# Turning x ahead of the first products over three bank pairs, and dummy products on PE at two places

## The chip, the cores and the metric

The kernel runs on one core of one Trainium2 chip. The metric is the device time of one execution in microseconds (us), the median of several runs. Engines are named as in the profile: PE is TensorE (PEld its weight loads), DVE is VectorE, ACT is ScalarE, POOL is GpSimd, SP is SyncE, which here only issues DMAs. An engine name with a q (PEq, ACTq) is that engine's sequencer.

## The reference

One layer of a decoder trunk, for a prompt of 256 tokens and 8 samples of one token each (264 columns in all), width 2048, all in float32:

```
x = x + 0.5 * SwiGLU_1(RMSNorm(x))          # 2048 -> 5632 twice, and back
h = RMSNorm(x);  P = h @ w_in               # 2048 -> 6400: attention, RWKV-7, gated conv
x = x + concat(attention, rwkv, conv) @ w_out
x = x + 0.5 * SwiGLU_2(RMSNorm(x))
```

The attention part is dilated sliding-window attention with 8 heads over cached keys and values. The RWKV-7 part is a delta-rule scan over the tokens with a state of 64x64 for each of 12 heads. After the scan each head's output `y` goes through a group norm (mean and variance over the 64 channels of the head), gets a per-head bonus added and is multiplied with a gate:

```
y = (y - mean(y)) * rsqrt(var(y) + 64e-5) * ln_w + ln_b
y_rwkv = (y + sum(r * k * r_k) * v) * g
```

Two ends of this matter here: the very beginning, where x is brought in and turned, and the end of the group norm, behind which the products with `w_out` start.

## The kernel before, in words

x is kept with its 2048 features on the partitions (16 tiles of 128) and the 264 tokens as columns, in `xr`. Every weight product is made in three passes, so that it is as exact as float32: weights and activations are each split into a head (`wH`, `xH`, rounded to fp32r, made by ACT) and a tail (`wL`, `xL`, the rest, made by DVE), and PE adds head x head, head x tail and tail x head (lines 324 to 326 in `products`). Weights come as chunks of four tiles of 128 rows by 256 columns (512 KB) through a ring of four buffers: SP's queue loads `raw` (line 297 in `load`), ACT makes the head (line 305 in `head`), DVE the tail (line 311 in `tail`), and PE has 24 products of 264 columns per chunk. The semaphores `tail_made` and `chunk_used` count chunks and let each stage run up to four chunks ahead.

The order of work of each engine is written out by hand, one program per engine, and each engine does its own in order.

The start. x comes from memory with tokens on the partitions (`xin`, four pieces of 512 features, and `xsin` for the samples), and PE turns it: `pe_turn_x(q)` transposes two tiles of features into two PSUM banks, with two large transposes (line 890) and a small one for the samples (line 891) each, against the identity in `cb`. There are eight such pairs q = 0 to 7. DVE copies a pair to `xr` (line 898 in `copy`), ACT makes its heads `xH` (line 359 in `x_heads`), DVE its tails `xL` (line 367 in `x_tails`). The two bank pairs 4, 5 and 6, 7 are used in turn, so turn q waits for the copy of pair q - 2; an even q also waits for its piece of x. ACT's queue loads four groups of small vectors (line 836), then `cb` (line 837) and `xsin` (line 838). SP's queue loads the four pieces of x (line 853), each followed by one weight chunk. PE turns pairs 0 to 3 (and the vectors, line 877), makes the first chunk of products, turns 4 and 5, makes the second chunk, turns 6 and 7, and goes on with the third.

The norm. x is normalised only after the product (a column of the result is scaled with the root of its sum of squares), so the sum of squares is not needed at first. ACT squares each pair (line 352 in `squares`), from behind the first four weight heads on, into two slots. POOL adds the squares up (lines 824 and 822 in `pool_squares`), one pair after the other. PE's `norm_sum` (lines 385 and 386) adds over the partitions with a matrix of ones. It stands behind the sixth chunk of the first pair of column tiles, and waits until POOL has added all eight pairs. ACT's root (393), DVE's reciprocal (398) and the first scaled gate (404) follow.

From there on, and in all the later projections, the products run as a stream.

The group norm's end. It works on two groups of columns: part 0 is the first 128, part 1 the other 136. PE sums over a head (2053), squares and sums (2064), spreads the root over the head's channels (2073); DVE centres, multiplies and adds in place in PSUM (2102 to 2105), ACT makes the mix's heads (2137) and DVE its tails (2141). PE's last piece of work there is `pe_group_spread` of part 1 (2073) and six transposes of the final state (2034), which ACT copies out (2190) behind two weight heads of the output projection. Then PE waits for the first weight tail of the output projection. The bonus sums of part 1 lie in banks 4 and 5 and are read by DVE's `dve_bonus_values` (2124), which counts `bonus_made`. The first products of the output projection write banks 4 and 5 too.

Of the kernel before, what the change touches and what calls it, by code (L numbers as in the profile page):

```python
# [23 lines left out]
P = 128  # L24
# [86 lines left out]
def build(nc, t, o):  # L111
# [597 lines left out]
    def pe_ffn(pe, u, gu, dn):  # L709
        w = 2 * u  # L710

        def gate_up(i, first_pair):
            for k in range(GU_PER):
# [4 lines left out]
                if k == 4 and not first_pair:  # L718
                    pe.wait_ge(S("up_scaled"), FT // 2 * u + i)
                products(pe, xH, xL, CK * (k % 4), CK, 0 if k < 4 else 2, k % 4 == 0, k % 4 == 3,  # L720
                         gu, GU_PER, i, k)
                if first_pair and u == 0 and k < 2:
                    pe_turn_x(pe, 2 * k + 4)
                    pe_turn_x(pe, 2 * k + 5)
                if first_pair and k == (5 if u == 0 else 3):
# [107 lines left out]
    def act_start(act):  # L833
        for name, r, n in (("ffn1_norm", "ffn1", 16), ("mix_norm", "mix", 16), ("ffn2_norm", "ffn2", 16),
                           ("rwkv_mu", "mu", 20)):
            act.dma_start(vrowa[VA[r]:VA[r] + n, :], row_view(name)).then_inc(S("base_in"), 16)
        act.dma_start(cb[:], t["c_base"]).then_inc(S("base_in"), 16)
        act.dma_start(xsin[:], t["x_sample"].rearrange("b s f -> (b s) f")).then_inc(S("x_in"), 16)
        act.wait_ge(S("constants_set"), 3)
        nc.scalar.activation(sd[:, 0:1], ep, ACT.Square)  # L840
        act.wait_ge(S("vectors_a_set"), 1)
        for k in range(RING):
            x_heads(act, 0, 2 * k)
            x_heads(act, 0, 2 * k + 1)
            head(act, CK, GU1, GU_PER, 0, k, fresh=True)
# [3 lines left out]
    def sp_start(sp):  # L849
        xp = t["x_prompt"][0].rearrange("(b p) f -> p b f", p=P)  # L850
        for k in range(RING):
            cols = slice(k * CK * P, (k + 1) * CK * P)
# [19 lines left out]

    def pe_start(pe):
        pe.wait_ge(S("base_in"), 16 * 5)
        pe.wait_ge(S("x_in"), 32)
        pe_turn_x(pe, 0)
        nc.tensor.transpose(ps[:, 0, 0:68], vrowa[:], ident[0:68, 0:68]).then_inc(S("vectors_a_turned"), 1)
        pe_turn_x(pe, 1)
        pe_turn_x(pe, 2)
        pe_turn_x(pe, 3)  # L880

    def pe_turn_x(pe, q):

        if q >= 2:
            pe.wait_ge(S("x_ready"), q - 1)
        if q % 2 == 0 and q:
            pe.wait_ge(S(X_IN[q // 2]), 16)
        for d in (2 * q, 2 * q + 1):
            for b in range(2):
                nc.tensor.transpose(ps[:, 4 + d % 4, b * P:b * P + P], xin[:, b, d * P:d * P + P], ident)  # L890
            last = nc.tensor.transpose(ps[:, 4 + d % 4, T:N], xsin[:, d * P:d * P + P], ident[0:NB, 0:NB])
        last.then_inc(S("x_turned"), 1)

    def dve_start(dve):
        def copy(q):
            dve.wait_ge(S("x_turned"), q + 1)
            b = 4 + 2 * (q % 2)
            nc.vector.tensor_copy(xr[:, 2 * q:2 * q + 2, :], ps[:, b:b + 2, 0:N]).then_inc(S("x_ready"), 1)
        copy(0)
        dve.wait_ge(S("vectors_a_turned"), 1)  # L900
        nc.vector.tensor_copy(vcol[:, 0, :], ps[:, 0, 0:68]).then_inc(S("vectors_a_set"), 1)
        dve.wait_ge(S("vectors_a_set"), 1)
        for k in range(RING):
            copy(2 * k + 1)
            x_tails(dve, 0, 2 * k)
            if k < RING - 1:
                copy(2 * k + 2)
            x_tails(dve, 0, 2 * k + 1)
# [1061 lines left out]
    def pe_chunks(pe):  # L1970
# [58 lines left out]
        pe_group_squares(pe, 1)  # L2029
        pe_group_spread(pe, 1)  # L2030
        pe.wait_ge(S("states_out"), 4)
        pe.wait_ge(S("head_root"), 3)
        for j in range(RT):
            last = nc.tensor.transpose(pf[0:C, 1024 + j * P:1024 + j * P + P], ST[:, j, :], ident)
        last.then_inc(S("state_turned"), 1)

    GROUP = ((slice(0, P), 0, 2), (slice(P, N), 6, 3))
# [352 lines left out]
```

## Time and profile before

| | us |
|---|---|
| median of 3 runs | 2142.46 (2138.77 to 2144.42) |
| the profiled execution | 2135.76 |
| its span, first to last instruction | 2133.9 |
| PE busy | 2076.6 (97%), weight loads 2042.1 |
| DVE, ACT, POOL busy | 1170.6 (55%), 880.8 (41%), 191.9 (9%) |
| mean granted TensorE clock | 0.992 of full |

A row of the windows gives the length of a stretch, then for each engine its busy time and in brackets how many instructions ran in it. A row of the timeline merges what repeats: start, time taken, engine, line, operation, output and inputs, how many, and in square brackets how long the engine was idle before it and what released it. A row of the waits sums up who waited for whom.

### The profile page before, as it was taken

Reading aid. Unit: us, or ns where it says so; the run is one execution under the profiler, and the core shown is the slowest. Engines: PE = TensorE matmul, PEld = TensorE weight load, DVE = VectorE, ACT = ScalarE, POOL = GpSimd, SP = SyncE. Lnnn points to the kernel's source line nnn. Section 1 sums busy time; section 2 is a strip of 40 time slices with the busy share of each in tenths; the row PEclk is TensorE's granted clock in tenths of the full one; section 3 lists DMA queues with packets and bytes.
Section 4 is the critical chain, followed back from the end, with each engine's and each line's share of the span. In section 5 each row is a group of like instructions: output and inputs, shape, how many; then the busy total and the mean of one; then the engine's idle time right before and its main releaser. Section 6 shows DMA issues by size and latency. Waiting matters only on the chain.

```text
span 2133.9 us, 44654 instructions
## 1 busy us (share of the span) xinstructions
PE 2076.6 (97%) x18392; PEld 2042.1 (96%) x18392; DVE 1170.6 (55%) x1203; ACT 880.8 (41%) x1004; POOL 191.9 (9%) x160
## 2 busy tenths in 40 slices
PE   6999999999999999999997979999999999999999
PEld 5999999999999999999985879999999999999999
DVE  4555555555545445568996555655555555544443
ACT  4443444434434434434345444444444444433333
POOL 3000000000000000014401860000000000000000
PEclk9999999999999999999998999999999999999999
DMA  5556555555555556668872045555555656556553
GB/s 162 178 179 185 178 184 179 178 186 177 182 173 178 187 170 198 177 201 219 245 229 61 4 153 183 179 181 181 182 178 180 183 179 184 178 162 201 181 182 123
DMA packets 361374, 373.41 MB, mean 175 GB/s; under 512 B 13321, under 2 KB 353837, under 8 KB 361190
## 3 DMA queue, kind: packets, MB, share of 16 engines
q1 hardware_dynamic: 352128, 350.33, 52.8%
q0 software_dynamic: 5424, 15.39, 3.0%
q10 hardware_dynamic: 3742, 6.52, 0.9%
q8 instruction: 62, 1.02, 0.2%
q14 instruction: 18, 0.15, 0.0%
HBM read 366.89 MB, written 5.32 MB: 174 GB/s over the span
## 4 chain that ended last, share of the span: by engine, by line
PE 88%; DVE 6%; DMA 2%; ACT 1%; issue 1%; POOL 1%; ACTq 1%; POOLq 0%; SPq 0%; DVEq 0%
PE ps L324 28%; PE ps L326 28%; PE ps L325 28%; DVE wL L311 2%; DMA raw<-in_w_in_dram 2%; POOL acc L822 1%; DMA vb<-in_cache_swa_v_dram 0%; PE ps L1878 0%; ACTq L1246 0%; PE ps L1875 0%; PE ps L1886 0%; PE ps L1186 0%; DMA xsin<-in_x_sample_dram 0%; DVE ss L1339 0%; ACT wH L305 0%
## 5 line engine op out<-in xcount | busy, mean ns | idle before, releaser
L311 DVE TENSOR_TENSOR wL<-raw,wH 128x1024 fp32r<-128x1024 f32 (+1 forms) x676 | 830.1, 1234 | 847.6 <-ACT wH L305 847.0
L305 ACT ACTIVATE wH<-raw 128x1024 fp32r<-128x1024 f32 (+1 forms) x676 | 699.8, 1037 | 979.6 <-PE ps L326 899.4
L324 PE MATMUL ps<-xH,wH 128*128 128x264 f32 x3616 | 1032.2, 285 | 8.8 <-DVE wL L311 8.7
L325 PE MATMUL ps<-xL,wH 128*128 128x264 f32 x3616 | 1028.9, 285 | 0.0
L326 PE MATMUL ps<-xH,wL 128*128 128x264 f32 x3616 | 1028.8, 285 | 0.0
L324 PEld LDWEIGHTS ps<-xH,wH 128*128 128x128 f32 x3616 | 683.1, 189 | 13.7 <-issue 12.6
L326 PEld LDWEIGHTS ps<-xH,wL 128*128 128x128 f32 x3616 | 682.7, 189 | 0.0
L325 PEld LDWEIGHTS ps<-xL,wH 128*128 128x128 f32 x3616 | 682.3, 189 | 0.2
L324 PE MATMUL ps<-hH,wH 128*128 128x264 f32 x1408 | 402.4, 286 | 0.0
L326 PE MATMUL ps<-hH,wL 128*128 128x264 f32 x1408 | 401.5, 285 | 0.0
L325 PE MATMUL ps<-hL,wH 128*128 128x264 f32 x1408 | 401.3, 285 | 0.0
L324 PEld LDWEIGHTS ps<-hH,wH 128*128 128x128 f32 x1408 | 265.0, 188 | 0.2
L325 PEld LDWEIGHTS ps<-hL,wH 128*128 128x128 f32 x1408 | 265.1, 188 | 0.0
L326 PEld LDWEIGHTS ps<-hH,wL 128*128 128x128 f32 x1408 | 264.6, 188 | 0.0
L324 PE MATMUL ps<-mixH,wH 128*128 128x264 f32 x256 | 73.6, 287 | 7.4 <-DVE wL L311 7.4
L325 PE MATMUL ps<-mixL,wH 128*128 128x264 f32 x256 | 73.4, 287 | 0.0
L326 PE MATMUL ps<-mixH,wL 128*128 128x264 f32 x256 | 73.3, 286 | 0.0
L408 ACT ACTIVATE st<-gt 128x528 f32<-128x528 f32 x44 | 28.5, 647 | 83.5 <-DVE gt L404 83.5
L822 POOL TENSOR_TENSOR acc<-acc,sq 128x528 f32<-128x528 f32 x21 | 34.1, 1622 | 287.4 <-ACT sq L352 286.4
L324 PEld LDWEIGHTS ps<-mixH,wH 128*128 128x128 f32 x256 | 48.9, 191 | 7.6 <-DVE wL L311 7.6
L824 POOL COPY acc<-sq 128x528 f32<-128x528 f32 x3 | 2.9, 973 | 574.5 <-ACT sq L352 574.5
L326 PEld LDWEIGHTS ps<-mixH,wL 128*128 128x128 f32 x256 | 48.9, 191 | 0.0
(365 smaller groups left out, 1030.1 us busy)
## 6 DMA issues: line engine op xcount, KB each, us to landing
raw<-in_ffn_w_gate_dram SPq DMA_DIRECT2D x176, 512.0 KB, 3.5
raw<-in_ffn_w_up_dram SPq DMA_DIRECT2D x176, 512.0 KB, 3.5
raw<-in_ffn_w_down_dram SPq DMA_DIRECT2D x128, 512.0 KB, 3.5
raw<-in_w_in_dram SPq DMA_DIRECT2D x100, 512.0 KB, 4.8
raw<-in_ffn_w_down_dram SPq DMA_DIRECT2D x64, 384.0 KB, 3.1
raw<-in_w_out_dram SPq DMA_DIRECT2D x32, 512.0 KB, 4.3
kb<-in_cache_swa_k_dram POOLq DMA_DIRECT2D x24, 256.0 KB, 6.5
vb<-in_cache_swa_v_dram ACTq DMA_DIRECT2D x24, 256.0 KB, 6.8
```

The costliest lines, as they stand in the source:

```text
L305: nc.scalar.activation(wH[:, k % RING, 0:nk, :], raw[:, k % RING, 0:nk, :], ACT.Copy).then_inc(S("head_made"), 1)
L311: nc.vector.tensor_tensor(wL[:, k % RING, 0:nk, :], raw[:, k % RING, 0:nk, :], wH[:, k % RING, 0:nk, :].bitcast(F32), ALU.subtract).then_i ...
L324: nc.tensor.matmul(out, wH[:, k % RING, q, cols], high, start=a, stop=False)
L325: nc.tensor.matmul(out, wH[:, k % RING, q, cols], low, start=False, stop=False)
L326: last = nc.tensor.matmul(out, wL[:, k % RING, q, cols], high, start=False, stop=b)
L408: nc.scalar.activation(st[:], gt[:], ACT.Silu).then_inc(S("silu_made"), 1)
L822: nc.gpsimd.tensor_tensor(acc[:], acc[:], sq[:, slot, :, :], ALU.add).then_inc(S("squares_added"), 1)
L824: nc.gpsimd.tensor_copy(acc[:], sq[:, 0, :, :]).then_inc(S("squares_added"), 1)
```

## The change

- The loads of `cb` and `xsin` leave ACT's queue and stand first on SP's, ahead of the pieces of x.
- PE starts with 32 dummy products of ones (256 columns of bfloat16, into bank 4), as soon as POOL has set the constants.
- PE turns pairs 0 to 5 ahead of the first chunk of products, and 6 and 7 behind it; nothing stands behind the second chunk. The turns use three bank pairs (2 and 3, 4 and 5, 6 and 7) in turn, so turn q waits for the copy of pair q - 3. DVE's copies are one pair further ahead of its tails.
- Behind the last spread of the group norm PE makes 8 dummy products, after a wait for DVE's bonus values, and 36 more behind the transposes of the state.

The dummies' results are never read. The whole diff:

```diff
--- before.py
+++ after.py
@@ -719,9 +719,9 @@
                     pe.wait_ge(S("up_scaled"), FT // 2 * u + i)
                 products(pe, xH, xL, CK * (k % 4), CK, 0 if k < 4 else 2, k % 4 == 0, k % 4 == 3,
                          gu, GU_PER, i, k)
-                if first_pair and u == 0 and k < 2:
-                    pe_turn_x(pe, 2 * k + 4)
-                    pe_turn_x(pe, 2 * k + 5)
+                if first_pair and u == 0 and k == 0:
+                    pe_turn_x(pe, 6)
+                    pe_turn_x(pe, 7)
                 if first_pair and k == (5 if u == 0 else 3):
                     norm_sum(pe, w)
 
@@ -834,8 +834,6 @@
         for name, r, n in (("ffn1_norm", "ffn1", 16), ("mix_norm", "mix", 16), ("ffn2_norm", "ffn2", 16),
                            ("rwkv_mu", "mu", 20)):
             act.dma_start(vrowa[VA[r]:VA[r] + n, :], row_view(name)).then_inc(S("base_in"), 16)
-        act.dma_start(cb[:], t["c_base"]).then_inc(S("base_in"), 16)
-        act.dma_start(xsin[:], t["x_sample"].rearrange("b s f -> (b s) f")).then_inc(S("x_in"), 16)
         act.wait_ge(S("constants_set"), 3)
         nc.scalar.activation(sd[:, 0:1], ep, ACT.Square)
         act.wait_ge(S("vectors_a_set"), 1)
@@ -848,6 +846,8 @@
 
     def sp_start(sp):
         xp = t["x_prompt"][0].rearrange("(b p) f -> p b f", p=P)
+        sp.dma_start(cb[:], t["c_base"]).then_inc(S("base_in"), 16)
+        sp.dma_start(xsin[:], t["x_sample"].rearrange("b s f -> (b s) f")).then_inc(S("x_in"), 16)
         for k in range(RING):
             cols = slice(k * CK * P, (k + 1) * CK * P)
             sp.dma_start(xin[:, :, cols], xp[:, :, cols]).then_inc(S(X_IN[k]), 16)
@@ -871,40 +871,54 @@
                 pool.dma_start(vrowb[VB[r]:VB[r] + 1, a * C:a * C + C], t[name]).then_inc(S("vectors_b_in"), 16)
 
     def pe_start(pe):
+        pe.wait_ge(S("constants_set"), 3)
+        pe_warm(4, 32)
         pe.wait_ge(S("base_in"), 16 * 5)
         pe.wait_ge(S("x_in"), 32)
         pe_turn_x(pe, 0)
         nc.tensor.transpose(ps[:, 0, 0:68], vrowa[:], ident[0:68, 0:68]).then_inc(S("vectors_a_turned"), 1)
-        pe_turn_x(pe, 1)
-        pe_turn_x(pe, 2)
-        pe_turn_x(pe, 3)
+        for q in range(1, 6):
+            pe_turn_x(pe, q)
+
+    def pe_warm(bank, count):
+
+        for _ in range(count):
+            nc.tensor.matmul(ps[:, bank, 0:2 * P], ones[:].bitcast(BF16)[:, 0:P], ones[:].bitcast(BF16),
+                             start=True, stop=True)
+
+    def turned_banks(q):
+
+        return 2 + q % 3 * 2
 
     def pe_turn_x(pe, q):
 
-        if q >= 2:
-            pe.wait_ge(S("x_ready"), q - 1)
+        if q >= 3:
+            pe.wait_ge(S("x_ready"), q - 2)
         if q % 2 == 0 and q:
             pe.wait_ge(S(X_IN[q // 2]), 16)
         for d in (2 * q, 2 * q + 1):
+            bank = turned_banks(q) + d % 2
             for b in range(2):
-                nc.tensor.transpose(ps[:, 4 + d % 4, b * P:b * P + P], xin[:, b, d * P:d * P + P], ident)
-            last = nc.tensor.transpose(ps[:, 4 + d % 4, T:N], xsin[:, d * P:d * P + P], ident[0:NB, 0:NB])
+                nc.tensor.transpose(ps[:, bank, b * P:b * P + P], xin[:, b, d * P:d * P + P], ident)
+            last = nc.tensor.transpose(ps[:, bank, T:N], xsin[:, d * P:d * P + P], ident[0:NB, 0:NB])
         last.then_inc(S("x_turned"), 1)
 
     def dve_start(dve):
         def copy(q):
             dve.wait_ge(S("x_turned"), q + 1)
-            b = 4 + 2 * (q % 2)
+            b = turned_banks(q)
             nc.vector.tensor_copy(xr[:, 2 * q:2 * q + 2, :], ps[:, b:b + 2, 0:N]).then_inc(S("x_ready"), 1)
         copy(0)
         dve.wait_ge(S("vectors_a_turned"), 1)
         nc.vector.tensor_copy(vcol[:, 0, :], ps[:, 0, 0:68]).then_inc(S("vectors_a_set"), 1)
         dve.wait_ge(S("vectors_a_set"), 1)
+        copy(1)
         for k in range(RING):
-            copy(2 * k + 1)
+            if k < RING - 1:
+                copy(2 * k + 2)
             x_tails(dve, 0, 2 * k)
             if k < RING - 1:
-                copy(2 * k + 2)
+                copy(2 * k + 3)
             x_tails(dve, 0, 2 * k + 1)
             tail(dve, CK, GU1, GU_PER, 0, k)
 
@@ -2028,11 +2042,14 @@
         pe_bonus(pe, 1)
         pe_group_squares(pe, 1)
         pe_group_spread(pe, 1)
+        pe.wait_ge(S("bonus_made"), 3)
+        pe_warm(4, 8)
         pe.wait_ge(S("states_out"), 4)
         pe.wait_ge(S("head_root"), 3)
         for j in range(RT):
             last = nc.tensor.transpose(pf[0:C, 1024 + j * P:1024 + j * P + P], ST[:, j, :], ident)
         last.then_inc(S("state_turned"), 1)
+        pe_warm(4, 36)
 
     GROUP = ((slice(0, P), 0, 2), (slice(P, N), 6, 3))
```

## Rows read from the trace of the kernel before

**Rows 1.** the page's chain that ended last, share of the span by engine

```profile
PE 88%; DVE 6%; DMA 2%; ACT 1%; issue 1%; POOL 1%; ACTq 1%; POOLq 0%; SPq 0%; DVEq 0%
```

**Rows 2.** the waits, 0 to 60 us: us in total, times, longest us

```profile
PE ps L890 <- DMA xsin<-in_x_sample_dram: 10.3, 1, 10.3
...
PE ps L324 <- DVE wL L311: 5.4, 4, 1.8
...
PE ps L385 <- POOL acc L822: 4.7, 1, 4.7
```

**Rows 3.** windows: stretch and length; busy us (instructions) by engine; PEclk, DMA share, GB/s

```profile
10.00:17.50 7.50, 6.72 (x25) 3.84 (x25) 4.40 (x9) 3.60 (x7) 0.00 (x0) 1.00 0.84 287
18.20:22.50 4.30, 4.25 (x24) 4.29 (x24) 1.32 (x3) 1.87 (x3) 0.00 (x0) 1.00 0.40 122
...
46.20:50.90 4.70, 0.00 (x0) 0.00 (x0) 2.86 (x2) 2.87 (x3) 4.41 (x4) 0.75 0.36 112
50.90:55.30 4.40, 4.40 (x16) 3.98 (x17) 1.72 (x1) 1.76 (x2) 4.40 (x9) 0.50 0.47 127
...
1252.90:1260.20 7.30, 0.02 (x1) 0.00 (x0) 6.13 (x7) 3.25 (x5) 6.64 (x4) 0.54 0.00 0
1260.20:1263.70 3.50, 3.42 (x15) 3.42 (x16) 2.39 (x3) 1.62 (x3) 0.09 (x1) 0.50 0.78 213
1263.70:1267.10 3.40, 3.40 (x30) 3.40 (x29) 1.72 (x2) 1.77 (x2) 1.27 (x2) 1.00 0.97 297
```

**Rows 4.** the chain that ended last, in order of time: start us, us, what

```profile
33.21 0.63 DVE xr L898
...
34.78 0.96 ACT wH L305
...
36.33 1.16 POOL acc L824
```

**Rows 5.** POOL's adds, line 822: duration ns min/median/max, first and last start

```profile
L822 POOL TENSOR_TENSOR acc<-acc,sq x7: 1308/2090/2115, 37.6 to 48.8; 128x528 f32<-128x528 f32 x7
```

**Rows 6.** DMA queues, 1.9 to 7.3 us: packets, MB, share of 16 engines

```profile
q10 hardware_dynamic: 134, 0.05, 3.3%
```

**Rows 7.** DMA queues, 7.3 to 9.1 us

```profile
q10 hardware_dynamic: 151, 0.19, 35.6%
```

**Rows 8.** timeline, 0 to 8 us: start us, us, engine line op out<-in

```profile
0.93 0.10 POOL L859 MEMSET eps<- 128x1 f32 x1
...
3.00 0.47 ACTq L837 DMA_DIRECT2D cb<-in_c_base_dram  x1
3.50 0.44 ACTq L838 DMA_DIRECT2D xsin<-in_x_sample_dram  x1
```

**Rows 9.** first weight loads, line 297, 0 to 3 us

```profile
DMA to landing us min/median/max: 5.7/7.2/8.7
```

**Rows 10.** the loads of x, line 853

```profile
L853 SPq DMA_DIRECT2D xin<-in_x_prompt_dram x4: 453/698/1555, 0.8 to 4.3; - x4
...
DMA to landing us min/median/max: 7.2/9.5/10.9
```

**Rows 11.** PE's timeline, 23 to 37.2 us (idle before it in brackets)

```profile
23.08 0.44 PE L890 MATMUL ps<-cb,xin 128*128 128x128 f32 x2
...
23.60 0.44 PE L890 MATMUL ps<-cb,xin 128*128 128x128 f32 x2
...
37.14 0.36 PE L324 MATMUL ps<-xH,wH 128*128 128x264 f32 x1 [0.62 <-DVE wL L311]
```

**Rows 12.** timeline at the end of the group norm

```profile
1250.52 1.62 PE L2073 MATMUL ps<-hn,hs 12*128 12x136 f32 x12 [1.88 <-DVE hn L2096]
...
1252.08 0.84 PE L2034 MATMUL ps<-cb,ST 128*64 128x128 f32 x6
...
1259.74 0.79 ACT L2190 ACTIVATE wkT<-ps 64x768 f32<-64x768 f32 x1
...
1260.29 0.59 PE L324 MATMUL ps<-mixH,wH 128*128 128x264 f32 x1 [7.37 <-DVE wL L311]
```

## The prediction

> **What bounds the kernel now.** I read the chain of waits first: TensorE (PE) takes 88% of the span [rows 1]. Almost all of it is a steady stream of weight products that nothing holds up, so a change can only win in the few stretches where PE idles or runs at the lower of its two clocks. The waits of the first 60 us show these stretches for the start [rows 2]: PE waits 10.3 us for its first input (the landing of x_sample), 5.4 us in four pieces for a weight tail from VectorE (DVE), and 4.7 us for GpSimd (POOL), which adds up the squares of x. The last is the one that ends last: all that PE loses before it is only seen if it moves the moment when POOL is done. The windows show it [rows 3]: 46.2 to 50.9 PE does nothing, and the next 4.4 us run at a granted clock of 0.50. The second place is 1252.9 to 1260.2, where PE idles behind DVE and ScalarE (ACT) at the end of the group norm, and then 15 records take 3.5 us at clock 0.50 where 30 take 3.4 us at 1.00.
>
> What sets POOL's end? Followed back along the chain [rows 4]: the last copy of x out of PSUM starts on DVE at 33.21, then ACT makes the last x heads and the weight head (34.78), squares the first pair, and POOL starts at 36.33, 3.1 us after that copy. From there it is a fixed train: one copy and seven adds, 1.31 to 2.12 us each [rows 5], until PE starts the norm sum at 50.9, 14.6 us later. The last copy is late because the turns (PE transposes) of x are split: two pairs stand behind the first chunk of products, two more behind the second. So the quantity to follow is the start of copy 7.
>
> **Part 1, the start.** The constants and x_sample move from the end of ACT's queue to the head of SP's. ACT's queue moved 0.05 MB by 7.3 us and 0.19 MB after it, to 9.1 [rows 6, 7]: the small vector rows first, then the two moved loads. PE started 1.2 us after 9.1. The vector rows stay where they are, so with the same 1.2 us they release PE at 8.5. The first piece of x is issued 0.47 + 0.44 = 0.9 us later than now [rows 8]; the first weight chunk, next behind it on the queue, landed 5.7 us after its issue at 1.3 [rows 9], so the piece would be there by about 8. I take 8.5; the ends are 7.5 and 10.3 (no gain). Everything else on SP's queue, weight loads included, is issued 0.9 us later too; the pieces of x land 7.2 to 10.9 us after issue [rows 10], the third at about 12.4 (issued near 2.9, the median), the last at 4.3 + 10.9 = 15.2, and are bound by bandwidth, so I leave these as they are. ACT gets to its table load 0.9 us earlier, which nothing needs.
>
> The 32 dummy products (256 columns, against 264 in a real one) cost 0.12 us at the high and 0.22 us at the low clock, so 3.8 to 7.0 us from about 1.1 us, where POOL's constants are ready [rows 8]. They end between 4.9 and 8.1, before 8.5: free, at either clock.
>
> Now six pairs are turned ahead of the products. A pair is two groups of two large and one small transpose. Before, eight groups and the vectors' own transpose (25 records) took 6.72 us at the low clock [rows 3], 0.82 a group (the clock column reads 1.00 there, ahead of its first change on record; the pace tells the level); at the high clock a group starts every 0.52 us [rows 11]. Twelve groups and the vectors' own transpose (0.2) are 6.4 to 10.0 us. I take 8.2, since I expect the dummies' clock to hold for part of them: PE is through at 16.7. DVE's first tail comes at about 16 and adds little; products start at 17.0 (range 16 to 18.5), against 18.2 now. The three bank pairs let PE run two turns ahead of the copies; with copies of 0.63 us against a pair's 1.04 to 1.64 that wait costs nothing.
>
> That row shows 6.72 us of PE busy with such transposes, and the products behind it still begin at the low pace: transposes don't raise the clock. The Trainium skill says more, in "TensorE: Matmul & The Clock Gate", Part 4 (PE-mode transpose): in that mode the full clock does not engage, since it is not counted as busy in the same way. By that rule the dummies' clock would be lost soon after the turns begin, and products would start nearer 18.5 and the whole come out 1 us worse than my sum; by the opposite reading it would come out 1.5 us better. No row of before shows long transposing from the high clock.
>
> The first chunk of 24 products took 4.3 us, part of it low [rows 3]; all high it is 3.0 (three chunks from 37.14 to 46.2 [rows 3, 11]), all low 5.3. I take 4.1: 21.1. Turns 6 and 7 are 4 groups at 0.52: 23.2. DVE copies pair 6, makes one pair of x tails (0.8), and starts copy 7 at 23.8 instead of 33.2. POOL starts at 26.9 and, after the same 14.6 us, would end at 41.5. But DVE's last x tails and third tail now fall beside POOL's first adds, and adds come in two sizes, 1.31 and 2.1 us; one more at the larger size is 0.8. Norm sum at 42.3 against 50.9: **8.6 us earlier**. For PE the chunks 1 to 5 (15.1 us and some 0.4 of waiting for the third tail) end at 38.7, so it idles some 3.6 us there instead of 4.7. The four waits for tails go, what is late next is POOL again. The 4.4 us at 0.50 behind the wait cost 2.2 us now; with a shorter wait and free chance when the clock falls I give back 0.6. Part 1: 9.2, with ends of 5 (late start, low clock) and 13 (high clock throughout). The loads of SP and POOL's vector loads behind the norm sum move along with it.
>
> **Part 2, the group norm.** Eight dummies stand behind the last spread (their wait on the bonus is met: DVE makes it ahead of the L2096 that released that spread [rows 12]) and ahead of the six state transposes: 1.0 to 1.8 us. The transposes then end near 1254 instead of 1252.9; who waits for them is ACT's L2190 at 1259.74, behind two heads: 5 us of cover, and PE itself waits until 1260.29. The 36 dummies then take 4.3 us at the high clock (to 1258.3) or 7.9 at the low (to 1261.9, 1.6 late). But the low clock would not last: the products that began at 1260.3 had it back at 1263.7. With 3.4 us low, 15 dummies, and 21 high they end at 1259.9. So no delay, and the gain is at most half of the 3.4 us at 0.50, 1.7 us. PE idles 2 us between the last dummy and the products if they ran high; a pause of 1.88 us before 1250.5 did not cost the clock at once [rows 12], one of 4.7 lost it [rows 3]. I take 1.1, ends -1.6 and +1.7.
>
> **Sum.** 9.2 + 1.1 = 10.3 us. The profiled execution took 2135.76 (span 2133.9 and 1.9 around it), so it would be 2125.5. The runs have a median of 2142.46, from 2138.77 to 2144.42, and the profiled one lies 6.7 below it; against the median the forecast is 2132. PE is bound by its own stream behind both places, so the gain should come through whole.
>
> **Rivals.**
> (B) The clock holds from the dummies on through the turns and PE starts at 7.5 to 8: products at 16, chunk 0 in 3.0, turns done at 21.1, copy 7 at 21.7, shift 10.7, and 1 to 2.2 from the stretch at 0.50: about 13 in all, 2129.5. For it: the high pace of turns exists. Against it: the 6.7 us of transposes that raised nothing.
> (C) The dummies of ones don't raise the clock, or it is gone at once: turns end at 18.5, chunk 0 in 4.3, turns 24.9, copy 7 at 25.5, shift 6.9 with the 0.8 of POOL, nothing at the second place: 2135.5. Against it: the dummies keep PE as dense as real products, which had the clock back after 3.4 us.
> (D) PE still starts at 10.3, because the vector rows or the first piece of x come no earlier, and all is low: 20.4, chunk 0 to 24.7, turns to 26.8, copy 7 at 27.4, shift 5: 2137.5. For it: the first piece of x now stands behind 0.19 MB.
> (E) Slower: PE is in order, and now turns 4 and 5, with their wait for the third piece of x, stand ahead of the first products. If cb and x_sample (7.3 and 6.8 us from issue to PE's start now) hold SP's queue one after the other, the third piece lands at 26.5 instead of 12.4; at the low clock two turns (3.3), the chunk (5.3) and two turns (3.3) put copy 7 at 39.0, 5.8 us later than now: about 2149. It decides from a landing at some 21 us on, every us later being one us. Against it: 0.19 MB went in 1.8 us once its turn came [rows 7].
>
> **How the numbers follow.** Forecast (A) 0.62, B 0.12, C 0.12, D 0.10, E 0.04. About 0.3% (6.4 us) is what a measurement of this kernel can tell from no change, so A's 10.3 is not far above it and the runs alone spread over 5.6. Chance of faster within each: A 0.88, B 0.97, C 0.6, D 0.35: together 0.77; slower is E and a little scatter, 0.04; the same 0.19. Range 2124.5 (A's sum on the profiled execution's level, and B) to 2139 (D and scatter); outside are E and the tails of D and of the runs.
>
> **What would show it.** First turn at about 8.5, dense dummies from 1.1; no PE wait for a DVE tail in chunk 1 and 2; copy 7 at about 24 and POOL's copy at about 27; norm sum at 42 with PE still waiting for POOL some 3 us; the products behind the group norm mostly at 0.28 and not 0.42 us each. I am wrong if PE's first turn is at 10 or later, if the turns run at 0.82 throughout, if POOL's train takes over 16 us, if a dummy ends after the first weight tail of the output projection, or if PE's stream behind the first pair has gained new waits.

## The result and the profile after

| | before | the change |
|---|---|---|
| median | 2141.27 (2138.77 to 2144.42, 4 runs) | 2124.58 (2121.88 to 2126.17, 4 runs) |
| profiled execution | 2135.76 | 2124.41 |

The ratio is 0.992, with a 95% interval from 0.9902 to 0.9938. The change is 16.7 us faster in the medians and 11.35 us in the two profiled executions. The forecast was 10.3 us. Its direction and its places were right, but the size was too small: the median lies at the lowest edge of the stated range, and the mean of the four runs, 2124.3, just below it.

From the page of the changed kernel, its span, its busy line and its chain:

```profile
span 2122.6 us, 44805 instructions
...
PE 2086.7 (98%) x18468; PEld 2048.7 (97%) x18468; DVE 1175.2 (55%) x1203; ACT 880.8 (41%) x1004; POOL 193.6 (9%) x160
...
PE 88%; DVE 6%; DMA 3%; ACT 1%; issue 1%; POOL 1%; ACTq 0%; SPq 0%; POOLq 0%; DVEq 0%
```

The waits of its first 55 us answer to [rows 2]:

```profile
PE ps L324 <- DVE wL L311: 2.4, 2, 2.1
...
PE ps L902 <- DMA xin<-in_x_prompt_dram: 1.2, 2, 0.8
PE ps L385 <- POOL acc L822: 1.2, 1, 1.2
```

The 10.3 us for the first input are gone, the four waits for weight tails (5.4) are two (2.4), and POOL holds PE for 1.2 us instead of 4.7. New are 1.2 us in which PE waits for two later pieces of x. PE's timeline of the first 20 us (start, length, instruction, how many) shows the new order:

```profile
1.08 6.13 PE L886 MATMUL ps<-ones 128*128 128x256 bf16 x32 [1.08 <-POOL eps L859]
7.05 0.38 PE L902 MATMUL ps<-cb,xin 128*128 128x128 f32 x2
...
12.54 0.41 PE L902 MATMUL ps<-cb,xin 128*128 128x128 f32 x2 [0.78 <-DMA xin<-in_x_prompt_dram]
...
13.03 0.69 PE L902 MATMUL ps<-cb,xin 128*128 128x128 f32 x2
...
15.49 0.59 PE L324 MATMUL ps<-xH,wH 128*128 128x264 f32 x1
```

The 32 dummies take 6.1 us, and the first turn follows at 7.05, against 10.34. A pair of large transposes takes 0.38 to 0.44 us up to the one at 12.54, and 0.69 from 13.03 on: there the clock falls. The products start at 15.49, against 18.25. The chain to the norm sum, answering to [rows 4] (start, length, what):

```profile
23.06 0.63 DVE xr L910
...
24.63 0.95 ACT wH L305
...
26.17 0.75 POOL acc L824
...
41.14 0.71 PE ps L385 x2
```

The last copy starts at 23.06 instead of 33.21, POOL at 26.17 instead of 36.33, the norm sum at 41.14 instead of 50.90. The windows, with PE's busy time first and the granted clock third from the end, answer to [rows 3]:

```profile
7.05:15.50 8.45, 7.29 (x40) 4.41 (x38) 6.30 (x12) 5.50 (x11) 0.00 (x0) 0.85 1.05 363
15.50:20.40 4.90, 4.90 (x25) 4.90 (x25) 3.30 (x6) 2.76 (x5) 0.00 (x0) 0.56 0.46 140
...
39.90:41.10 1.20, 0.09 (x1) 0.00 (x0) 0.04 (x1) 0.00 (x0) 1.20 (x2) 1.00 0.81 277
1242.30:1244.00 1.70, 1.70 (x10) 1.20 (x10) 0.69 (x1) 0.81 (x1) 1.62 (x2) 0.50 0.07 22
...
1250.40:1253.90 3.50, 3.47 (x28) 3.47 (x29) 2.34 (x2) 1.96 (x3) 0.39 (x1) 1.00 0.83 242
```

PE is idle for 1.2 us ahead of the norm sum and keeps the clock. Behind the group norm 28 records now go into 3.5 us at clock 1.00, where 15 did at 0.50. PE's timeline there, answering to [rows 12]:

```profile
1240.52 1.85 PE L2090 MATMUL ps<-hn,hs 12*128 12x136 f32 x12 [1.88 <-DVE hn L2113]
1242.31 1.89 PE L886 MATMUL ps<-ones 128*128 128x256 bf16 x8
1243.99 1.41 PE L2050 MATMUL ps<-cb,ST 128*64 128x128 f32 x6
1245.24 4.09 PE L886 MATMUL ps<-ones 128*128 128x256 bf16 x36
1250.43 0.39 PE L324 MATMUL ps<-mixH,wH 128*128 128x264 f32 x1 [1.10 <-DVE wL L311]
```

And the last copy out of PSUM, on DVE, in the profile after and in the chain of before:

```profile
2117.28 0.71 DVE L632 SCALAR_TENSOR_TENSOR yf<-ps,xr 128x528 f32<-128x528 f32 x1 [6.95 <-PE ps L326]
```

```profile
2128.66 0.72 DVE yf L632
```

From the first product of the output projection to this copy it is 868.37 us before (2128.66 - 1260.29) and 866.85 after (2117.28 - 1250.43): 1.5 us for the second place. I use the same difference for the experiments below.

The stretches of the two profiled executions add up. The norm sum comes 9.8 us earlier. The stretch behind it is shorter by 1.6: the last of the gate and up scalings that I compared starts 57.79 us behind the norm sum before (108.69 - 50.90) and 56.19 after (97.33 - 41.14). The output projection gives 1.5. That is 12.9, and 11.4 remain at the last copy: from that scaling to the first product of the output projection the change takes 1.5 us longer.

### The profile page after: what moved, and what is told of

The parts are those of the page before. It is cut to its first block, busy times and chain, and to the rows that moved or that the text cites. A ratio compares the mean times of both kernels' runs of the same rounds, so it can differ in the third digit from the quotient of the medians.

```text
span 2122.6 us, 44805 instructions
## 1 busy us (share of the span) xinstructions
PE 2086.7 (98%) x18468; PEld 2048.7 (97%) x18468; DVE 1175.2 (55%) x1203; ACT 880.8 (41%) x1004; POOL 193.6 (9%) x160
## 4 chain that ended last, share of the span: by engine, by line
PE 88%; DVE 6%; DMA 3%; ACT 1%; issue 1%; POOL 1%; ACTq 0%; SPq 0%; POOLq 0%; DVEq 0%
PE ps L324 28%; PE ps L326 28%; PE ps L325 28%; DVE wL L311 3%; DMA raw<-in_w_in_dram 2%; POOL acc L822 1%; DMA vb<-in_cache_swa_v_dram 0%; DMA xin<-in_x_prompt_dram 0%; PE ps L1892 0%; PE ps L1889 0%; PE ps L1200 0%; PE ps L1900 0%; ACT wH L305 0%; ACTq L1260 0%; DVE ss L1353 0%
```

## The experiments

All times are compared with the kernel before in the same session (medians 2139.2 to 2140.9). "By the ratio" means: the ratio of the two kernels' runs, times some 2140 us. Two theories were set against each other. Theory P says that the two profiled executions compare fairly and the rest of the 16.7 us is scatter. Theory M says that the kernel before loses more in most executions than in the one the forecast used. M was later split in M1 (two terms of my sum were too small) and M2 (2 to 3 us come from the middle of the kernel). "New order" stands for the turns over three bank pairs, with or without the rest of the change.

**Before, timed and profiled again** (no edit).

> The kernel before, once more, for a second profile of it. Theory P (the two profiled executions compare fairly, 11.3 us between them, and the rest of the 16.7 us between the medians is scatter): its profiled execution lands between 2136 and 2144, the norm sum starts near 51 in it, and where it is above 2136 the extra lies in stretches at granted clock 0.50 in the middle of the kernel, away from both places of the change. Theory M (the kernel before loses more in most runs than its profiled execution shows, at the places of the change): the norm sum starts later than 51, at 53 to 56, or the products behind the group norm lose more than 1.7 us.

2140.84 (11 runs; ratio 1.0004, 0.9995 to 1.0013). The norm sum started at 52.94, 2.0 us later than in the first profile, though PE's first turn came 0.2 us earlier, and the second chunk began at the low pace. That is M's sign (M had put it at 53 to 56) and not P's.

**Before, three more profiled executions** (no edit).

> The kernel before, one more profiled execution. If the first profile was the exception, the norm sum starts at 52 to 54 here and the chunks ahead of it are partly at 0.42 us a record; if it was the rule, at 50.7 to 51.2.

> As the one ahead of it: 52 to 54 if the first profile was the exception, 50.7 to 51.2 if it was the rule.

> As the two ahead of it. With all six the mean start of the norm sum is 52.3 to 53 if the early clock loss explains 1.5 to 2 us of what the forecast missed.

They took 2137.71, 2137.71 and 2137.49, with the norm sum at 50.80, 54.20 and 51.66. PE's timeline of the second of them: the first products of the second and the third chunk, and the norm sum.

```profile
27.05 0.56 PE L324 MATMUL ps<-xH,wH 128*128 128x264 f32 x1 [1.79 <-DVE wL L311]
...
36.66 0.56 PE L324 MATMUL ps<-xH,wH 128*128 128x264 f32 x1 [1.79 <-DVE wL L311]
...
54.20 1.25 PE L385 MATMUL ps<-acc,ones 128*128 128x264 f32 x2 [4.18 <-POOL acc L822]
```

The products behind both waits for a tail begin at the low pace (0.56 for the first record instead of 0.36 [rows 11]). The pauses are 1.79 us long in all of these executions, and the clock survives them in some and not in others. Of six executions with this order of turns (these three, the first profile, the one above, and the one with only the late dummies at 54.11) two are at 50.8 to 50.9, the others at 51.7 to 54.2. The mean is 52.4, as expected (52.3 to 53). One by one the three fell on both sides: 50.80 in the range of "the rule", 54.20 just above that of "the exception", and 51.66 between them. The forecast had started from one of the two best.

**Dummies in PE's pauses, nothing reordered.**

```diff
                     pe_turn_x(pe, 2 * k + 5)
+                    pe_warm(2, 12)
...
+                if first_pair and u == 0 and k == 5:
+                    pe_warm(4, 36)
```

> The kernel before with dummies only where PE idles in its first 51 us: 12 behind turns 4 and 5, 12 behind turns 6 and 7, 36 ahead of the norm sum. Nothing is reordered. Theory M1: the chain to the norm sum is then as in the best case, 51 in every execution, and the products behind it are high: 1.8 + 2.2 = 4 us faster than before, 2137. Rival (the clock in this stretch is worth no more than the forecast's 0.6 us, the rest of the gain is the order of the turns): within 1 us of before.

2137.23 (11 runs; ratio 0.9987, 0.9978 to 0.9996): 2.9 us faster.

```profile
24.39 1.48 PE L879 MATMUL ps<-ones 128*128 128x256 bf16 x12
26.25 0.36 PE L324 MATMUL ps<-xH,wH 128*128 128x264 f32 x1 [0.37 <-DVE wL L311]
...
45.74 4.11 PE L879 MATMUL ps<-ones 128*128 128x256 bf16 x36
50.66 0.71 PE L385 MATMUL ps<-acc,ones 128*128 128x264 f32 x2 [0.81 <-POOL acc L825]
```

The norm sum is at 50.66, as in the best case, and is itself at the high pace (0.71 instead of 1.25). So the clock of these 55 us alone is worth some 3 us to a kernel that reorders nothing. That is nearer to the 4 I expected than to the rival's 1, but the interval (0.9 to 4.7 us) reaches down to the rival.

**Only the moved loads.**

```diff
-        act.dma_start(cb[:], t["c_base"]).then_inc(S("base_in"), 16)
-        act.dma_start(xsin[:], ...).then_inc(S("x_in"), 16)
...
+        sp.dma_start(cb[:], t["c_base"]).then_inc(S("base_in"), 16)
+        sp.dma_start(xsin[:], ...).then_inc(S("x_in"), 16)
```

> Only the two loads moved to the head of SP's queue. PE's first turn at 7 us instead of 10.1, everything behind it as before: products at 14.9 to 16 (DVE's tail needs the weights of the first chunk, landed by 8), so the chain to the norm sum is 2.5 to 3.1 us shorter: 2137.5 to 2138 against 2140.5. The forecast's step (8.5, held back by the vector rows on ACT's queue): 1.8 us, and a first turn at 8.5.

2136.23 (12 runs; ratio 0.9985, 0.9972 to 0.9997): 3.0 us faster. First turn, first product, norm sum:

```profile
6.70 0.66 PE L890 MATMUL ps<-cb,xin 128*128 128x128 f32 x2 [6.70 <-DMA xin<-in_x_prompt_dram]
...
14.61 0.56 PE L324 MATMUL ps<-xH,wH 128*128 128x264 f32 x1 [1.19 <-DVE wL L311]
...
47.59 1.25 PE L385 MATMUL ps<-acc,ones 128*128 128x264 f32 x2 [4.77 <-POOL acc L822]
```

The first turn comes at 6.70 and is released by x, not by the vector rows: the step "8.5, held back by ACT's queue" was wrong. The whole 3.6 us (10.34 - 6.70) arrive at the first product (18.25 - 14.61).

**Only the turns over three bank pairs** (loads as before, no dummies).

> Only the turns over three bank pairs, with the six pairs ahead of the products; loads as before on ACT's queue, no dummies anywhere. First turn near 10.1, twelve groups at 0.82 us, turn 5 ends near 20.2, the first chunk half low, copy 7 near 26.5 to 28, norm sum at 44.5 to 46. Theory M1: the wait ahead of it is under 2 us, so the clock holds there: 6.5 + 2 us faster than the kernel before, 2132. The forecast's own sum (0.6 us for that clock): 6.5 us, 2134.5.

2133.13 (6 runs; ratio 0.9971, 0.9958 to 0.9983): 7.0 us faster.

```profile
10.86 0.66 PE L900 MATMUL ps<-cb,xin 128*128 128x128 f32 x2 [10.86 <-DMA xsin<-in_x_sample_dram]
...
46.25 0.71 PE L385 MATMUL ps<-acc,ones 128*128 128x264 f32 x2 [1.16 <-POOL acc L822]
```

From first turn to norm sum it is 35.4 us, against 40.6 in the first profile of before. PE waits 1.16 us for POOL here too, and the clock is at 1.00 behind it. This is the largest single part. The time lies between M1's 8.5 us and the 6.5 us of the forecast's own sum, and the interval (3.6 to 9.0 us) holds both, so it doesn't choose.

**Moved loads and turns, no dummies.**

> The moved loads and the new order of turns, no dummies anywhere. First turn at 6.9, norm sum at 42.8 as in the kernel without the early dummies, then the group norm's end as before (products low for about 3 us): 9.8 us shorter to the norm sum against the average of before, 2.2 us kept clock behind it: 12 us in all, 2128.5. If the early and the late dummies each gain 5 us as single removals suggest, it is at 2134 instead.

2129.00 (6 runs; ratio 0.9951, 0.9937 to 0.9964), norm sum at 42.83: the level and the norm sum as expected. The gain is 10.5 us by the ratio (7.7 to 13.5) where 12 were expected, and the 7.0 and 3.0 of the two parts add up to about that. One row of its profile was not foreseen:

```profile
32.62 0.56 PE L324 MATMUL ps<-xH,wH 128*128 128x264 f32 x1 [2.15 <-DVE wL L311]
```

Here the clock was lost in the pause of 2.15 us ahead of the fourth chunk (granted clock 0.50 from 32.6 to 35.8), and PE reached the norm sum with no idle time left ahead of it.

**The change without its early dummies.**

```diff
-        pe.wait_ge(S("constants_set"), 3)
-        pe_warm(4, 32)
```

> The change without the 32 dummies at the very start; queue, turns and the end as in the change. Theory P: PE's first turn comes when its inputs are there (7 to 8.5 us), all twelve groups are at 0.82 us, turn 5 ends at 17 to 18.5, copy 7 starts near 24.5 instead of 23.0, the norm sum near 42.5 instead of 41.1: 1.5 us above the change, 2126 (2 to 3 us more if PE then idles long enough ahead of the norm sum to lose the clock). A rival (the early dummies do nothing that lasts, since the clock was gone by 12.9 anyway): the same as the change within 0.7 us.

2129.51 (5 runs; ratio 0.9948), 5 us above the change where 1.5 was expected. First turn:

```profile
6.88 0.66 PE L900 MATMUL ps<-cb,xin 128*128 128x128 f32 x2 [6.88 <-DMA xin<-in_x_prompt_dram]
```

It is 0.2 us earlier than in the profile with the dummies, which so cost a little, but all twelve groups are low. The norm sum is at 42.77, 1.6 later than in the change, as expected. The end of the group norm shows another 1.5:

```profile
1247.36 4.09 PE L884 MATMUL ps<-ones 128*128 128x256 bf16 x36
1254.00 0.59 PE L324 MATMUL ps<-mixH,wH 128*128 128x264 f32 x1 [2.54 <-DVE wL L311]
```

```profile
1251.50:1253.95 2.45, 0.00 (x0) 0.00 (x0) 2.23 (x3) 2.45 (x4) 1.90 (x2) 1.00 0.00 0
1253.95:1257.40 3.45, 3.40 (x15) 3.41 (x16) 2.35 (x2) 1.55 (x3) 0.02 (x1) 0.51 0.83 229
```

The late dummies all ran high here, ended 2.54 us ahead of the products, and the clock fell as the products began: 15 records in 3.4 us. From there to the last copy it is 868.36 us, as without any dummies. In the change the 36 took the same 4.09 us. What ran low there were the 8 dummies ahead of them (1.89 us instead of 1.05) and the state's transposes (1.41 instead of 0.82), and these 1.4 us are the difference between a pause of 1.10 and one of 2.54. So the late dummies helped only where what stands ahead of the 36 ran low. The remaining 2 us of the 5 lie, in the profiled execution, between the norm sum and the output projection, which no edit touched: 1211.2 us, against 1209.3 in the change.

**Before with the late dummies alone.**

```diff
+        pe.wait_ge(S("bonus_made"), 3)
+        pe_warm(4, 8)
         pe.wait_ge(S("states_out"), 4)
...
         last.then_inc(S("state_turned"), 1)
+        pe_warm(4, 36)
```

> The kernel before with the 8 and 36 dummies at the end of the group norm and nothing else. Theory P: 1.1 us faster than before, between 0 and 2 (2139 to 2141 against 2141). Theory M with its loss there: 3 to 5 us faster.

2139.16 (11 runs; ratio 0.9993, 0.9984 to 1.0002): 1.5 us by the ratio, in the range of P, but not clear of zero. Its profiled execution had the idle time of 2.54 us and 868.35 behind it: no gain in that one.

**The change without the late dummies**, run twice.

```diff
-        pe.wait_ge(S("bonus_made"), 3)
-        pe_warm(4, 8)
...
-        pe_warm(4, 36)
```

> The change without the 8 and 36 dummies at the end of the group norm. Theory P: 1.7 us above the change as a whole at most, 0 to 3 us in the medians, so 2125 to 2128, with the products behind the group norm at the low clock for 1 to 4 us. Theory M with its loss at the second place: 3 us or more above the change as a whole.

> The change without its late dummies, a second time, to tell 5 us from 2. The rows behind the first product of the output projection (866.85 us to the last copy with the dummies, 868.4 to 869.1 without) give 1.5 to 2.2: 2126 to 2126.5. If it is at 2129 to 2130 again, some 3 us more hang on these dummies, and they lie ahead of them.

2129.66 and 2125.77 (5 runs each). The first seemed to give the late dummies 5 us, the second 1.2. The mean of all ten is 2127.3, 3.1 above the mean of the change's nine, and the rows give 2.2 and 2.5 (869.06 and 869.36 to the last copy, against 866.85). The second time was as expected, so nothing ahead of the dummies hangs on them that I can show. Five runs with a spread of 3 to 5 us don't size a term of 2.

**The change once more.**

> The change as it is, timed and profiled once more. Theory M1 (two terms of the forecast's sum were too small: the kernel before loses the clock already between its first chunks in most executions, 2 us more on average than in the one the forecast used, and the shorter idle time ahead of the norm sum keeps the clock, 2.2 us): 13.5 to 15 us faster than before, so 2126 to 2127, with the norm sum between 41.0 and 41.6. Theory M2 (the first 16.7 us are the true size, and 2 to 3 us of it come from somewhere in the middle of the kernel): 2124 to 2125 again.

2124.54 (5 runs; ratio 0.9929, 0.9916 to 0.9943). The norm sum was at 41.43 and the last copy 866.85 us behind the first product. The 2124 of the first measurement came again, which is M2's number, and M1's level (2126 to 2127) is 1.5 to 2.5 us too high. Against before it is 15.2 us by the ratio (12.2 to 18.0), so M1's gain of up to 15 is not excluded. That the rest comes from the middle of the kernel, as M2 has it, is not shown.

**46 late dummies instead of 36.**

> The change with 46 instead of 36 dummies behind the state's transposes. Theory G (the dummies end too early: where they ran at the high clock PE idles 2.5 us behind them and the products begin low all the same): PE's idle time ahead of the output projection is at most 1.5 us, its products run at the high clock from the first on, 0.5 to 1 us faster than the change in the median. Rival (36 were enough in most executions): the same, or up to 0.5 us slower where the dummies run low and end behind the first weight tail.

2127.32 (5 runs; ratio 0.9937). Its profiled execution had no pause ahead of the output projection and kept the clock, as theory G says: 866.85 us to the last copy, the same as in the change's two profiles. The median is 2.8 us above the change in the same session, which neither theory expected. In the profile the stretch from the norm sum to the first product of the output projection took 1212.2 us, against 1209.3 and 1206.3 in the two profiles of the change, and that stretch has no edit in it. For the total the run decides nothing.

**Dummies in the two waits for x.**

```diff
         for q in range(1, 6):
+            if q in (2, 4):
+                pe_warm(1, (6, 12)[q // 4])
             pe_turn_x(pe, q)
```

> The change with 6 more dummies ahead of turn 2 and 12 more ahead of turn 4, in the two waits for pieces of x (0.4 and 0.8 us), so that the clock does not fall during the turns. Theory K (the low clock from 12.9 to 19.7 costs the chain to the norm sum: 0.3 us for each of 3 groups and half of 4.1 us of products, less 0.6 us that the dummies overrun the wait): turn 5 ends near 15, the first chunk takes 3 us, norm sum 1.5 to 2.5 us earlier than in the change, 2122. Rival (transposing loses the clock whatever stands between, or DVE's tails bound the chain by then): norm sum within 0.5 us of 41.2 or later, the median at 2124 to 2125.

The windows over turns and first chunk, and PE's rows:

```profile
7.60:15.80 8.20, 8.19 (x55) 5.68 (x55) 5.80 (x11) 5.47 (x10) 0.00 (x0) 1.00 1.04 359
15.80:20.90 5.10, 5.10 (x37) 4.33 (x37) 4.74 (x9) 2.98 (x6) 0.00 (x0) 1.00 0.41 128
```

```profile
9.74 0.83 PE L888 MATMUL ps<-ones 128*128 128x256 bf16 x6
...
12.49 1.48 PE L888 MATMUL ps<-ones 128*128 128x256 bf16 x12
...
39.81 0.61 PE L385 MATMUL ps<-acc,ones 128*128 128x264 f32 x2
```

The clock stays at 1.00 through the turns, where the change has 0.85 and 0.56, and the norm sum comes at 39.81, 1.3 to 1.6 us earlier. The median is 2124.56 (6 runs), the same as the change: in its profile PE idled 2.53 us behind the late dummies and lost the 1.5 us there. The place was right, the total was the rival's.

The gain at the norm sum, too, is only at the low end of what theory K expects, and the profile shows what ate the rest: behind the 2.14 us of waiting for the tail of the fourth chunk the clock fell after all.

```profile
29.49 0.36 PE L324 MATMUL ps<-xH,wH 128*128 128x264 f32 x1 [2.14 <-DVE wL L311]
...
30.97 0.42 PE L326 MATMUL ps<-xH,wL 128*128 128x264 f32 x1
```

It was at 0.50 from 30.8 to 34.2, and the norm sum followed PE's last product without a pause: here PE's own stream and no longer POOL sets it.

**Both: dummies in the waits for x, and 46 late ones.**

> The change with the 6 and 12 dummies between the turns and 46 instead of 36 at the end. If both edits add up where their rows show a gain: norm sum at 39.8 (1.5 us earlier), PE idle ahead of the output projection under 1.5 us in every execution and its products high from the first, where the change loses up to 1.5 us in the executions in which its 36 dummies all run high: 1.5 to 2.5 us faster than the change, 2122 to 2123. Rival (the middle of the kernel takes it back, as it did with the norm sum's 1.5 us in the single edit): 2124 to 2125, the same as the change.

2120.82 (2119.26 to 2124.65, 5 runs; ratio 0.9915, 0.9901 to 0.9929), against 2140.93. The norm sum:

```profile
38.95 0.61 PE L385 MATMUL ps<-acc,ones 128*128 128x264 f32 x2
```

and the group norm's end:

```profile
1239.33 6.16 PE L888 MATMUL ps<-ones 128*128 128x256 bf16 x46
1245.28 0.39 PE L324 MATMUL ps<-mixH,wH 128*128 128x264 f32 x1
```

The norm sum is at 38.95, the first product follows the last dummy without a pause and at the high pace, and it is 866.85 us to the last copy. Here too the clock fell behind the wait for the fourth tail (0.50 from 29.6 to 33.0). This beats the kernel before by 18.2 us by the ratio (15.2 to 21.2) and 20.1 by the medians. The change was 15.6 to 16.7 faster than before by the medians, but the two were never timed in one session and their intervals overlap, so a gain of some 1 to 4 us over the change is suggested, not shown.

## Why the prediction was right and where it was wrong

**The order of the chain was right.** I followed the last copy of x to POOL's start (3.1 us, 3.11 measured), POOL's train (15.4 with one more long add; 15.0 measured) and the norm sum. Copy 7 was put at 23.8 and came at 23.06, the norm sum at 42.3 and came at 41.14. The dense dummies from 1.1, chunk 1 without a wait and chunk 2 with 0.3 us of it (I had allowed 0.4) and the high pace behind the group norm came as written; the first turn at 8.5 and the 3 us of waiting for POOL did not.

**"They release PE at 8.5" was wrong.** I let the vector rows keep the landing they had while two larger loads were queued behind them. ACT's queue from 1.9 to 5.5 us in the profile after (packets, MB, share):

```profile
q10 hardware_dynamic: 125, 0.04, 4.2%
```

By then all its rows were moved; before, it had moved 0.02 MB in that stretch. First turns came at 6.48 to 6.88 without dummies, released by x. With dummies they came at 6.83 to 7.62, so "free" was off by up to 0.7 us. The first turn was 1.45 us earlier than forecast. The first chunk, which took 4.96 us instead of 4.1, ate part of that, and copy 7 came 0.7 earlier than forecast.

**The clock of the turns.** I took 8.2 us, the middle between all groups high (6.4) and all low (10.0). From first turn to first product it took 8.44, but not as I had summed it: nine of the twelve groups ran high and only three low, and 1.16 us are waits for two pieces of x, which my sum had at nothing. That the total fits is in part luck. Without the early dummies all twelve groups and the vectors' transpose, 9.9 us without a listed pause, stayed low, so transposes alone didn't raise the clock. With the dummies it fell 6 us after the first turn, with PE busy for 7.29 of 8.45 us, and with 18 more dummies in the two waits it held at 1.00. The Trainium skill's sentence on PE-mode transposes ("TensorE: Matmul & The Clock Gate", Part 4), that the full clock does not engage in that mode, fits both rows only in part: while the clock was high, the transposes did run at the high pace (0.44 us against 0.69). That it is the transposes that lose the clock, and not the two waits that the 18 dummies also filled, is not shown. What I made of the rule in full, products nearer 18.5, did not come: they began at 15.49.

**"PE idles some 3.6 us there", and with it the 0.6 us for the clock behind that wait, is the step of the mechanism that failed.** I saw that DVE's tails would fall beside POOL's adds, but priced the collision for POOL alone (0.8 us). DVE pays as well. Its tails beside the adds (min/median/max ns), after and before:

```profile
L311 DVE TENSOR_TENSOR wL<-raw,wH x5: 1632/2322/2336, 28.6 to 38.3; 128x1024 fp32r<-128x1024 f32 x5
```

```profile
L311 DVE TENSOR_TENSOR wL<-raw,wH x4: 1605/1932/2285, 37.8 to 48.1; 128x1024 fp32r<-128x1024 f32 x4
```

Tails in this stretch take up to 2.34 us instead of 1.22, and the four x tails ahead of the fourth chunk's tail take 3.14 us together instead of some 1.7 (the longest 1.55 instead of 0.48). So the fourth tail starts at 28.59, takes 2.32, and PE waits 2.15 us for it, until 31.06. That both engines slow each other is read from their rows lying side by side; no run took one of them away. In the change's two profiles the wait costs nothing at the norm sum, since POOL ends last there. It eats idle time: PE is through at 39.98, 1.3 us later than forecast, and POOL is done 1.16 us earlier, so 1.16 us of idle time are left of the 3.6. In all seven profiles in which PE idled 4.2 to 4.8 us ahead of the norm sum (the old order) about 3 us or more at clock 0.50 stood at it or right behind it. In the ten with the new order, with 1.2 us or none, and in the one whose wait was filled with dummies, it was at 1.00. So the 4.4 us at clock 0.50 are gone whole. I had given them 0.6 us and they gave 1.6. Whether a pause of 3.6 us would have lost the clock no run shows.

**The base was wrong.** The first profile kept the clock through both pauses of 1.79 us. In three of six it was lost in at least one of them, in a fourth it rose later in the first chunk, and the mean norm sum is at 52.4. (A seventh execution, the one with only the moved loads, kept it through both.) The new order has neither of these pauses, so it gains 1.5 us on average that the one execution could not show; this was the largest single miss that I can place. It has the pause of 2.15 us ahead of the fourth chunk instead, and behind that one the clock fell in three of its ten profiles, though in none of the change itself. I had written that the clock falls by chance, but used chance only behind the norm sum.

**The sum again.** Norm sum 52.4 to 41.3 (mean of the change's two profiles): 11.1 instead of 8.6. Clock behind it 1.6 instead of 0.6. Output projection 1.5 instead of 1.1. Together 14.2 instead of 10.3. The profiled executions agree: 2137.3 for before (mean of five) and 2123.1 for the change (of two) are 14.2 apart. Two of the terms are less sure than this looks. The 1.6 us stand in every profile just behind the norm sum (56.1 to 56.2 us to the scaling compared above with the new order, 57.2 to 58.6 with the old), but over the whole stretch to the output projection the ten profiles of the new order are only 0.5 us shorter on average than the seven of the old one without dummies in its pauses (1209.5 and 1210.0). And the 36 late dummies kept the clock in two of the five profiles that had them; those two are the change's own. The timed ones are 16 apart, because the five profiled ones of before lie 3 us below its timed mean of 2140.5. Why is open.

**Level.** The forecast set 2132 against the median and kept the profiled execution's level (2125.5) only as an edge of the range. The edge turned out right, though for another reason: not that the level was 6.7 lower (the median of before was 1.2 lower, 2141.27), but that the gain was 6 us larger.

## What to carry to other kernels

Where the clock is lost behind a pause in some executions and not in others, as behind the 1.79 us here, one profile is one draw: take several and price the term by their mean. When two engines collide, price both, and ask what the slower one does to the idle time in front of the next wait, since a shorter pause can be worth more than the time it takes away. The new pause that the slower engine makes must be priced too: here it cost the clock in three of ten profiles.

Dummy work on PE should be sized for the case in which it runs at the high clock, and must reach up to the real work. 36 dummies that ended 2.5 us early gained nothing that shows in those executions (868.35 to 868.39 us behind them, within the 868.15 to 869.63 of the eleven profiles without them).

## What the runs showed that I had not expected

- A pause of PE of 2.53 or 2.54 us behind the dummies was followed by 3.4 us of low clock in all three executions that had it (early dummies removed, late dummies alone, dummies in the waits for x); pauses of 1.04 and 1.10 us, and none at all, were followed by the high clock.
- The length of a pause alone did not decide. Behind 1.79 us the clock was lost in three of seven executions, behind 2.15 us at once in one of ten and 1.0 to 1.3 us later in two more; and in one profile of before the norm sum behind 4.17 us of idle time still ran at the high pace (0.71), and the clock fell 1 us later.
- DVE's tail of 128x1024 takes 1.22 us alone and up to 2.34 beside a POOL add of 128x528, which itself goes from 1.31 to 2.13.
- The stretch from the norm sum to the first product of the output projection, which no edit touched, took between 1206.3 and 1212.2 us. The low stretches there sit in other places in each execution. Between the change's two profiles it differs by 3.0 us, and the executions by 2.7. That it makes most of a median's spread of 5 us is likely, not shown.
